# Merge, projection and norm of later token groups moved beside the expert gathers of the current group

## What is computed

```python
def _merge(oa, ob, oc, gates, wa, wb, wc, wo):
    ga, gb, gc = jnp.split(jax.nn.sigmoid(gates), 3, axis=-1)
    y = ga * (oa @ wa) + gb * (ob @ wb) + gc * (oc @ wc)
    return y @ wo
...
def _peer(h, w_q, subkeys, u_tab, v_tab):
    q = (h @ w_q).reshape(t, PEER_HEADS, 2, PEER_QDIM // 2)
    s = jnp.einsum('thid,hind->thin', q, subkeys)
    s_top, i_top = lax.top_k(s, PEER_TOPK)
    ...                       # top 16 of the 16x16 sums: idx, gate, for each of 8 heads
    act = gelu(einsum('td,thkd->thk', hb, u_tab[ib]))
    return einsum('thk,thkd->td', gb * act, v_tab[ib])
...
        x = x + mx[2] * mix_x
        hx = _modulate(_rmsnorm(x, norm2_g[l]), mx[3], mx[4])
        fx = _peer(hx, peer_w_q[l], peer_subkeys[l], peer_u[l], peer_v[l])
        x = x + mx[5] * fx
```

## Time and profile before

| | us |
|---|---|
| median of 3 runs (6759.11 to 6768.72) | 6765.36 |
| the profiled execution | 6770.41 |
| its span | 6768.6 |
| PE busy | 5562.9 (82%) |
| DVE busy | 3232.7 (48%) |
| ACT busy | 1679.4 (25%) |
| POOL busy | 1287.7 (19%) |
| gathers | 1280, 1342.26 MB |

### The profile page before, as it was taken

The page is one execution under the profiler, slowest core; times in us unless marked ns, Lnnn a source line. Parts: engine busy times, 40 slices in busy tenths (PEclk is TensorE's granted clock), DMA queues, the critical chain, the costliest instruction groups (busy, mean ns, idle before and its releaser), DMA issues. The chain is left out here.

```text
span 6768.6 us, 54389 instructions
## 1 busy us (share of the span) xinstructions
PE 5562.9 (82%) x18084; PEld 2922.8 (43%) x18084; DVE 3232.7 (48%) x7126; ACT 1679.4 (25%) x4406; POOL 1287.7 (19%) x1284
## 2 busy tenths in 40 slices
PE   6989987999888777777777787999799788777777
PEld 2488644555444333333332234985344333333322
DVE  1357205201366766676764324660231266766654
ACT  1410124200222332223232223100430133332322
POOL 0000000000133333333333200000000133433333
PEclk8989998999899999999999998989799899999999
DMA  6000010211488999999999840001022398999998
GB/s 194 28 1 0 31 45 4 56 42 39 168 304 302 422 421 414 419 415 415 419 417 420 335 140 12 1 0 52 28 56 56 122 353 336 421 421 421 421 420 355
DMA packets 372133, 1510.07 MB, mean 223 GB/s; under 512 B 61266, under 2 KB 173012, under 8 KB 207572
## 3 DMA queue, kind: packets, MB, share of 16 engines
q0 software_dynamic: 184320, 1342.26, 48.7%
q1 hardware_dynamic: 152020, 160.19, 7.4%
q10 hardware_dynamic: 35584, 5.12, 0.5%
HBM read 1505.38 MB, written 2.10 MB: 223 GB/s over the span
## 5 line engine op out<-in xcount | busy, mean ns | idle before, releaser
L1522 PE MATMUL ps<-ring,diag 128*128 128x512 f32 x5120 | 2422.9, 614 | 742.9 <-ACT diag L1439 733.5
L1398 POOL DMA_INDIRECT ring<-peer_uv,picks x1280 | 1287.5, 1006 | 5442.8 <-DVE picks L1625 3335.8
L1642 DVE CUSTOM_DVE_ANT_0 ring<-ring,hn 128x1024 f32<-128x1024 f32 x1280 | 1561.2, 1223 | 1002.2 <-DMA ring<-peer_uv,picks 998.4
L1522 PEld LDWEIGHTS ps<-ring,diag 128*128 128x128 f32 x5120 | 944.1, 193 | 2128.1 <-ACT diag L1439 1134.5
L1428 ACT ACTIVATE acts<-dots 128x2 f32<-128x2 f32 x640 | 130.1, 203 | 2052.5 <-DVE dots L1642 2052.3
L1439 ACT ACTIVATE diag<-consts,wgt 128x128 f32<-128x128 f32 x1280 | 445.0, 394 | 23.9 <-PE ps L1522 2.9
L1185 PE MATMUL ps<-hT,wg 128*128 128x512 f32 (+1 forms) x1152 | 427.6, 528 | 17.9 <-DMA wb<-w_branch_c 11.0
L1502 PE MATMUL ps<-hT,wq 128*128 128x512 f32 (+1 forms) x768 | 317.5, 536 | 8.5 <-DMA wq<-peer_wq 8.5
L1432 ACT ACTIVATE wgt<-gates,acts 128x1 f32<-128x1 f32 x1280 | 308.0, 287 | 61.1 <-ACT acts L1428 2.2
L1185 PEld LDWEIGHTS ps<-hT,wg 128*128 128x128 f32 x1152 | 220.0, 192 | 220.2 <-issue 209.9
L801 PE MATMUL ps<-hT,w 128*128 128x512 f32 (+1 forms) x832 | 297.5, 518 | 20.0 <-DMA w<-w_in 16.1
(11 more groups left out here) (267 smaller groups left out, 5639.5 us busy)
## 6 DMA issues: line engine op xcount, KB each, us to landing
w<-w_mod SPq DMA_DIRECT2D x24, 2048.0 KB, 7.9
w<-w_in SPq DMA_DIRECT2D x28, 1024.0 KB, 5.3
wg<-w_in SPq DMA_DIRECT2D x48, 512.0 KB, 6.0
ring<-peer_uv,picks POOLq DMA_INDIRECT x1280
wq<-peer_wq SPq DMA_DIRECT2D x32, 512.0 KB, 6.0
w<-w_in SPq DMA_DIRECT2D x4, 2048.0 KB
w<-w_out SPq DMA_DIRECT2D x8, 1024.0 KB, 6.0
mixing<-mixing_dram ACTq DMA_DIRECT2D x2, 2432.0 KB, 9.5
```

Of the source, the lines that this page charges most:

```text
L1398: pool.indirect_dma_start(out=ring[:, n % S, :], out_offset=None, in_=table, in_offset=bass.IndirectOffsetOnAxis(ap=picks[:, half(i), p:p ...
L1522: last = pe.matmul(ps[:, total_bank(i), 512 * b:512 * (b + 1)], diag[:, n % DIAGS], ring[:, n % S, D + 512 * b:D + 512 * (b + 1)], start=( ...
L1642: dve.tensor_tensor_reduce(out=row, in0=row, in1=hn[:, half(i)], scale=1.0, scalar=0.0, op0=ALU.mult, op1=ALU.add, accum_out=dots[:, half( ...
```

## The change

The ring becomes 6 slots in both layers. Tokens go through the end of a layer in groups of 256 (two tiles): three groups in layer 0, two in layer 1. Merge, `w_out`, residual and norm of the first group run alone (`mix_alone`); those of every later group are written by the same generator, `mix_group`, into the instruction lists of `experts`, beside the gathers of the group ahead of it. Its work is cut into units: unit 1 and 2 the norm of `ycT`, units 3 to 26 the 24 merges (12 matmuls of 256 columns each), 27 to 34 the blocks of `w_out`, 35 the sum of squares, 36 to 43 the norm. `plan` says at which pick (slot, counted 0 to 255 in a group) a unit is due, and every engine runs its part of the unit at the end of that slot. In the even (first) tile a unit is due every 7.1 slots (merges 0 to 14 at slots 28, 35, 42, ... 127), from slot 128 on every 2.1 slots (merges 15 to 23 at 128 to 144, the `w_out` blocks at 146 to 161, the norm up to 181).

Queries are made per group (256 columns), in a ring of 6 blocks `qpT`, the keys in a ring of 3. Six query blocks stand ahead of the first dot; the first six of a later group are made in the last 64 slots of the group ahead. Of each even tile 15 picks (p%8 == 7) and of each odd tile 30 (p%4 == 3) have their v row added on DVE into `vacc` instead of on PE; `total` adds `vacc` in at the end. Only one PSUM pair is left for the sum, and PE runs `accumulate` in pairs at odd p. Weights of merge and `w_out` are laid out in blocks on the host (786 KB for a merge, 524 KB for a `w_out` block). SBUF addresses are given by hand.

```diff
-RING = (7, 9)
+GROUP = 2 * P
+RING = 6
...
+class Beside:
+    def advance(self, slot):
+        for j, (plan, program) in enumerate(self.plans):
+            due = plan(slot)
+            if due and self.begun[j] is None:
+                self.begun[j] = 0
+                self.begun[j] = next(program, 1 << 30)
+            while due and self.begun[j] < due:
+                self.begun[j] = next(program, 1 << 30)
...
+    def mix_group(self, s, l, at, branches, yT, sq, earlier=None):
...
+        def tensor_program(pe):
...
+            for m in range(MERGES):
+                yield FIRST + m
+                pe.wait_ge(loaded[m % 2], 16 * (m // 2 + 1))
...
+                if m >= 2:
+                    pe.wait_ge(taken, m - 1)
+                for k in range(KD):
+                    pe.matmul(bank(m)[:, 0:G], w[:, m % 2, k], self.hT[:, k, tok], start=(k == 0), stop=(k == KD - 1))
+                for k in range(HB):
+                    last = pe.matmul(bank(m)[:, G:2 * G], w[:, m % 2, KD + k], branches[m % 3][:, k, tok], start=(k == 0), stop=(k == HB - 1))
+                last.then_inc(multiplied, 1)
+            for b in range(KD):
+                yield OUT + b
...
+                if b:
+                    pe.wait_ge(added, b)
+                for k in range(KD):
+                    last = pe.matmul(bank(0)[:, 0:G], w[:, n % 2, k], yT(k), start=(k == 0), stop=(k == KD - 1))
+                last.then_inc(multiplied, 1)
...
+        def scalar_program(act):
...
+            for m in range(MERGES):
+                yield FIRST + m
+                act.wait_ge(multiplied, m + 1)
+                if m >= 2:
+                    act.wait_ge(taken, m - 1)
+                act.activation(sg[:, m % 2], bank(m)[:, 0:G], ACT.Sigmoid).then_inc(opened, 1)
...
+        def vector_program(dve):
...
+            for m in range(MERGES):
+                yield FIRST + m
+                dve.wait_ge(opened, m + 1)
...
+                dve.tensor_tensor(to, sg[:, m % 2], bank(m)[:, G:2 * G], ALU.mult).then_inc(taken, 1)
...
+            for b in range(KD):
+                yield OUT + b
+                dve.wait_ge(multiplied, MERGES + b + 1)
+                dve.scalar_tensor_tensor(self.xT[:, b, tok], bank(0)[:, 0:G], self.modT[:, 2 * KD + b, kind:kind + 1],
+                                         self.xT[:, b, tok], ALU.mult, ALU.add).then_inc(added, 1)
...
-            self.merge(l, 1.0 - lam_init, oaT, ybT, ycT, yT, lo)
-            self.add_mixed(l, yT, lo)
+        self.mix_alone(l, lo, (oaT, ybT, ycT))
+        self.experts(l, lo, (oaT, ybT, ycT))
...
+        LAG = 4
...
+            def on_vector(r, p):
+                return p < 120 and (p % 8 == 7 if r % 2 == 0 else p % 4 == 3)
...
                 def _(pool):
...
+                                if n - S in vector_order:
+                                    pool.wait_ge(vadded, vector_order[n - S] + 1)
+                                elif n >= S:
+                                    pool.wait_ge(used[n % S], tensor_uses[n - S])
...
+                    def add_row(n):
+                        r, p, j = n // PICKS, n % PICKS, vector_order[n]
+                        row, weight = ring[:, n % S, D:2 * D], wgt[:, r % 2, p:p + 1]
+                        dve.wait_ge(weighted, n // 2 + 1)
...
+                            last = dve.scalar_tensor_tensor(vacc[:, :], row, weight, vacc[:, :], ALU.mult, ALU.add)
+                        last.then_inc(vadded, 1)
...
+                        dot(r, p)
+                        if slot >= LAG and (slot - LAG) in vector_order:
+                            add_row(slot - LAG)
+                        side_stages.advance(slot)
...
+                        for n in (p - 1, p) if p % 2 else ():
+                            if not on_vector(r, n):
+                                accumulate(r, n)
+                        if p == PICKS - 1:
+                            total(r)
+                        if step := query_step(slot):
+                            query(*step)
+                        side.advance(slot)
```

More of the change, by code:

```diff
@@ L1203, in _ @@
[L1203 to L1209 removed]
+                    finish(mix.scalar(act))
@@ L1231, in add_mixed @@
[L1231 to L1248 removed]
+                    finish(mix.vector(dve))
@@ L1311, in experts @@
         before = list(self.gathered_counts)
-        for n in range((end - first) * PICKS):
+        for n in range(R * PICKS):
             self.gathered_counts[n % S] += 16
@@ new lines, in plan, with due @@
+            def plan(g):
+                units, a = mixes[g - 1].units, (g - 1) * SLOTS
+                early, last = 18, SLOTS - 74
+                def due(slot):
+                    n = slot - a
+                    if n < 0:
+                        return 0
+                    if n < PICKS:
+                        return (n + 1) * early // PICKS
+                    return min(units, early + (n - PICKS + 1) * (units - early) // (last - PICKS) + 1)
+                return due
+            plans = [plan(g) for g in range(1, NG)]
@@ new lines, in experts, with choice, query_step @@
+            tensor_uses = {n: sum(m in tensor_order for m in range(n % S, n + 1, S)) for n in tensor_picks}
+            def choice(r, kb):
+                g, second = r // 2, r % 2
+                if not second:
+                    return NB * g + (0 if kb == 0 else 2 * kb - 1)
+                return NB * g + (2 * kb + 2 if kb < PH - 1 else NB - 1)
+            def query_step(slot):
+                g, n = slot // SLOTS, slot % SLOTS
+                if n < KD * (NB - 6):
+                    return g, 6 + n // KD, n % KD
+                n -= SLOTS - 64
+                if 0 <= n < 6 * KD and g + 1 < NG:
+                    return g + 1, n // KD, n % KD
+                return None
@@ L1524, in accumulate, with total @@
                         last.then_inc(used[n % S], 1)
[L1525 to L1532 removed]
+                    def total(r):
+                        pe.wait_ge(vadded, sum(m < (r + 1) * PICKS for m in vector_picks))
+                        for b in range(2):
+                            last = pe.matmul(ps[:, 1, 512 * b:512 * (b + 1)], ident, vacc[:, 512 * b:512 * (b + 1)], start=False, stop=True)
+                        last.then_inc(totalled, 1)
@@ L1568, in _, with choose @@
+                    turn_sum(R - 1)
                 @block.vector
                 def _(dve):
+                    side_stages = beside([m.vector(dve) for m in mixes])
                     step = Steps(dve, chosen)
-                    def choose(i, kb, part):
-                        c = choice(i, kb)
+                    def choose(r, kb, part):
+                        c, half = choice(r, kb), r % 2
                         scores = sc[:, c % 2]
```

736 lines of the change are left out of this document (402 added, 334 removed).

## The result

The changed kernel takes 7853.79 us (median of 4 runs, 7849.01 to 7857.95) against 6766.97: ratio 1.1608, 95% interval 1.1588 to 1.1629. It is slower, as forecast, but by 1087 us where 520 were forecast, and over the upper end of the range (7640). The profiled execution took 7857.95, its span 7856.2.

What follows compares the result with a forecast made beforehand. PE bounds each layer's start, DMA gathers the tiles. Tiles of 3 x 957 + 2 x 807 = 4485 us against 3427.5 add 1057; less 521 serial and some 20 overlap gives 7285 us, range 6980 to 7640.

Steps and rivals of the forecast that it cites:

- vector rows: Ring slots held for DVE's row add: each row idles the DMA engines 3.1 to 4.1 us, taken as 3.4.
- units: Mix beside gathers: DVE waits for PE, 9.5 us each; 8 us per even-tile merge, 11.5 us per odd-tile merge round.
- the 12 us for the choices: Even tiles: 12 us added for DVE, whose choices take 7.3 us each.
- (B): Expert tiles: units stall but vector rows are hidden; 6736 us in all, chance 0.03.
- Serial part: Layer start up to the first gather: 215 us instead of 558 and 393, saving 521 us together.
- The two-buffer rule: Mix run alone: two weight buffers make two merges take at least 6.0 + 5.2 us, so 5.6 each.
- Queries: First tiles: 256-column groups end PE's bound, and DVE's wait for scores inside the tiles is taken as gone.
- The forecast's rule: Tile time from gathers: 321 us by the DMA rate, plus 12 for DVE in the even tile.
- The ring: Six slots: returns by PE still 1 to 2 us early, so the shorter ring alone costs nothing in a quiet tile.
- (A): Expert tiles: vector rows stall but units cost nothing, PE being ahead; 6856 us in all, chance 0.05.
- (C): Expert tiles: both waits hidden and only DMA bytes count; 6281 us in all, chance 0.05.
- (D): ACT stalls add 3 us on each of 96 units, vector rows cost 4.1; 7700 us, chance 0.13 for above 7600.

Runs made afterwards that it cites:

- e1: Changed kernel with no v rows added on DVE, all on PE again; 7100.92 us.
- e10: Changed kernel with every group's mix run alone ahead of the gathers, no v rows on DVE, and a ring of 7 instead of 6; 6669.61 us.
- e7: Kernel before the change with a ring of 6 slots in both layers instead of 7 and 9; 6879.28 us.
- e3: Changed kernel with every group's mix run alone ahead of the gathers and no v rows on DVE, ring still 6; 6790.21 us.
- e5: Changed kernel with mix units run two slots later on ACT and three later on DVE than on PE; 7368.36 us.
- e2: Changed kernel with every group's mix run alone ahead of the gathers, v rows still on DVE; 7760.97 us.
- e6: Changed kernel with v rows added two dots late instead of four, and units two slots later on ACT, three on DVE; 6656.84 us.
- e9: Changed kernel with units two slots later on ACT and three on DVE, and no v rows on DVE; 6621.97 us.
- e4: Changed kernel with each v row added on DVE two dots after its own instead of four (LAG 2); 7151.99 us.

## Why the prediction was right in direction and short in size

The miss in the tiles is 5048 − 4465 = 583 us, and e1 splits it: quiet tiles 165 (3399 where the forecast has 3234), vector rows 137 (758 for 621), units 246 (891 for 645), and 35 that the forecast had taken off for overlap of the two and for rounding. (Of the 165, 36 are a slip in the sum: the 12 us for the choices, which the quiet even tile and rival (B) have, are left out of the three even tiles with a mix.)

**Serial part: right.** 549 against 521. From merge's start to the first gather 200 us pass in layer 0 where 215 were forecast. The two-buffer rule was a little dear: the 24 merges follow each other every 5.2 us, the time of their matmuls, and not every 5.6.

**Queries: right in direction, 6 us a tile short.** The first tile fell from 444.4 to 342.4 us with seven slots (e10), and DVE's wait for scores over the kernel from 297.6 to 47.6 us in the changed kernel. The forecast's rule gives 333 us for an even tile and 321 for an odd one. Over e10's ten tiles the sum is 3328 against 3270 by that rule.

**The ring: wrong.** The step that failed reads "with six slots and 5.3 to 6.3 to land these are still 1 to 2 us early, so the shorter ring alone costs nothing in a quiet tile". The arithmetic was right for the row it used. But a margin of 1 to 2 us covers an undisturbed round only, and the kernel before had issues lengthened by a dot as well (12 in its third tile), with one dot late. e7 and e10 against e3 give 112 and 121 us for it, some 12 us a tile: most of the 165. That these delays are how the ring costs is argued, as said at run 7; that it costs is shown.

**Vector rows: right mechanism, mis-sized.** POOL's issues come in bursts behind a wait for `vacc`, the issue stands 2.70 us behind the dot (2.8 forecast), and the quiet odd tile has a DMA share of 0.73 (0.76 forecast). Two terms were short. "5.3 to 6.3 to land", taken near the short end: the usual burst needs 6.25, since its first issue starts within a dot (25 of 30 bursts of the last odd tile of layer 0) and then takes 1.8 us. And "nothing makes it up, since the following ones come at the 2.5 us rate": the second gather of a burst comes 3.7 us behind the first (median of that tile, 2.8 to 4.8). Together a row of the quiet odd tile costs 4.8 instead of 3.4.

**Units: the wait right, its cover wrong.** 9.2 us per merge beside gathers against 9.5 forecast. But the even tile was said to hide 1.5 us of each in a cycle of 7.1 slots, and e1 measures 162 us per even tile for its units against 125 forecast. Nothing is hidden there: DVE's waits for the sigmoid sum to 158 to 161 us in these tiles. In the odd tile the round takes 13.5 us in the mean, against 11.5 ("pair 2.6 on the mean"): the pair was priced at the clock of a tile without waits. e1 measures 135 there against 90. e5 confirms the mechanism: without the wait, 147 of the 202 us per group go.

**The rivals.** (A), units free, and (B), rows free, fall with e2 and e1: each alone costs 840 to 968 us. (C) is what the change would be without both waits; e6 and e9 come to 6657 and 6622, not to its 6281. (D), "more than forecast", was nearest at 7700 and had 0.13. Its rows at 4.1 and its 3 us more per unit are near what happened (4.8 in the quiet odd tile, 246 over 96 units is 2.6). Whether ACT in `take_query`, the place it named, has a part in it was not tested. The range failed because its upper end took each term at its worst row of the kernel before, and the clock and the ring's margin were in none of them.

The Trainium skill ("DMA: Bandwidth & Descriptors", section on the anatomy of one DMA, SWDGE path) makes a gather of this size 4.4 us by its fit, and by that figure the change would have cost 224 us less than forecast (220 by the forecast's own counts of rows). The trace agrees with it only from the end of the issue: from there to the dot the bursts of the two quiet odd tiles take 4.5 us in the median. From the start of the issue, which is what the round needs, it is 5.4 us in the first burst above and 6.25 in the usual one, so the forecast was right not to use 4.4. The Trainium skill ("SBUF — State Buffer", section "SBUF: two separate sides") has a rule that the forecast left out and that would have moved it upward: a VectorE instruction with two SBUF inputs and a GpSimd instruction that reads SBUF exclude each other, and the one that starts second is blocked until the first is done. A dot has two SBUF inputs, and the issue of a gather reads `picks`. The trace agrees for an issue behind a dot, and not for a dot behind an issue, with numbers below.

## What to carry to other kernels

Interleaving two chains in lists that are executed in order pays only if the consumer's step stands later in its list than the producer needs. The same unit on three engines "in the same slot" is a full stop of the last engine; two and three slots of distance turned a ratio of 1.057 into 0.984 (e4 to e6). In a ring of buffers price each change by when a slot comes back, not by the work: a row of 1.28 us cost 4.8 because it gave the slot back two dots too late, and one slot less cost 1.6% though each round looked covered by 1 to 2 us. Price a step behind a wait at the time it has behind a wait: the same eight matmuls took 3.70 in a tile without waits and 5.10 here.

## What the runs showed of the hardware

**A gather's issue on POOL is held up by a dot that is already running.** Alone it takes 0.93 to 0.94 us. Of the 75 issues that start within a dot in the last two tiles of layer 0 of the changed kernel, 67 end 0.80 to 0.83 us after the end of that dot, whenever they began (so 0.94 to 2.0 us long). The other eight start in the dot's first 0.01 us or its last 0.1 us and take their usual 0.94. In the second tile of the kernel before it is all 6, in the third of e7 32 of 35. In the rows above: the dot of 4223.76 ends at 4224.98, the issue of 4224.00 at 4225.80; the dot of 4210.08 ends at 4211.31, the issue of 4210.92 at 4212.11. An issue that starts just ahead of a dot isn't lengthened, nor is the dot (issue 2608.48 with 0.94, in the same tile in which dots take 1.23): in the kernel before 650 dots start while an issue runs, and all of them take 1.20 to 1.25 us. Nor does every DVE instruction do it: of the 42 issues that start within a MAX8 of L1785, which reads one tile, none takes over 1.0 us.

**An idle DMA queue doesn't restart at its rate.** In the last odd tile of layer 0 the first gather of a burst takes 5.4 to 6.6 us from issue to dot, the second comes 2.8 to 4.8 behind it (median 3.7), the later ones mostly 2.5. What holds up the second is open.

**The granted clock falls in tiles full of waits**: 0.75 in the quiet odd tile (PE busy 53%) and 0.80 in that with a mix, of 1.00 before. The Trainium skill ("TensorE: Matmul & The Clock Gate", Part 1) describes two levels, 1.2 GHz after idling and 2.4 when busy; the timeline agrees: in the accumulate of 1957.85, behind 3.41 us of idle time, the weight loads first take 0.33 us and follow each other every 0.86, then take 0.19 and follow every 0.43, half of it. Raising it by filling (0.90) brought 61 of 1087 us, with the quiet tiles among what got shorter; removing the waits (0.95 to 0.97 in the tiles of e9) brought it back by itself.
